# A slot table for the experts: six indirect scatters to DRAM and one load in place of products of one-hot maps

## The reference

```
probs = softmax(hf @ w_router)
topv, topi = top_k(probs, 2);  topv = topv / sum(topv)
gates = sum(one_hot(topi, 8) * topv[..., None], axis=1)
for e in range(8):
    out = out + gates[:, e:e+1] * swiglu(hf, w_gu_e[e], w_down_e[e])
swiglu(h) = (silu(g) * u) @ w_down,  g, u = split(h @ w_gu)      # w_gu 1024 x 5632, w_down 2816 x 1024
```

## Time and profile before

| | |
|---|---|
| median of 3 runs | 1412.44 us (1411.51 to 1413.75) |
| span of the profiled execution, first to last instruction | 1408.6 us |
| mean granted TensorE clock | 0.986 of full |
| PE busy | 1351.2 us, 96% of the span |
| DVE, ACT, POOL busy | 1117.5 (79%), 811.1 (58%), 238.1 (17%) us |
| share of TensorE in the chain that ended last | 88% |

### The profile page before, as it was taken

One profiled execution on the slowest core, in us unless ns is written; L12 is line 12 of the kernel. 1 busy time (PEld: TensorE's weight loads), 2 busy tenths in 40 slices (PEclk: granted clock), 3 DMA queues, 4 the chain that ended last, 5 costly groups with the idle time before them and its releaser, 6 DMA issues.

```text
span 1408.6 us, 17000 instructions
## 1 busy us (share of the span) xinstructions
PE 1351.2 (96%) x6717; PEld 1126.3 (80%) x6717; DVE 1117.5 (79%) x1031; ACT 811.1 (58%) x812; POOL 238.1 (17%) x338
## 2 busy tenths in 40 slices
PE   4999989999999998989999999999999999999996
PEld 2787557799999986788888888888888888888884
DVE  2698766567676656658899899998998999989997
ACT  4432764423232224255777777777777777767773
POOL 4000681000000013001999200000000000000001
PEclk9999999999999999989999999999999999999998
DMA  9967444854554437537899999999999999999991
GB/s 312 378 228 268 134 144 163 312 196 151 180 179 163 166 147 245 196 135 290 288 401 388 363 412 371 381 388 355 414 375 372 412 348 397 386 355 406 369 413 53
DMA packets 119238, 409.75 MB, mean 291 GB/s; under 512 B 8385, under 2 KB 31090, under 8 KB 102258
## 3 DMA queue, kind: packets, MB, share of 16 engines
q1 hardware_dynamic: 111376, 382.24, 72.2%
q0 software_dynamic: 6704, 23.14, 5.4%
q10 hardware_dynamic: 1074, 3.23, 0.6%
HBM read 398.58 MB, written 9.99 MB: 290 GB/s over the span
## 4 chain that ended last, share of the span: by engine, by line
PE 88%; POOL 4%; DVE 3%; DMA 2%; ACT 1%; issue 1%; SPq 1%; POOLq 0%; DVEq 0%; ACTq 0%
PE ps L1814 26%; PE ps L1816 26%; PE ps L1815 26%; DMA raw<-in_ada_w 2%; PE ps L2196 1%; POOL xn L725 1%; POOL o_rstd L723 1%; DVE ring_lo L1612 1%; PE ps L2096 1%; POOL o_msq L721 1%; PE ps L2038 1%; PE ps L2139 1%; SPq L502 1%; PE ps L2169 1%; DMA gbc<-in_cache_v 0%
## 5 line engine op out<-in xcount | busy, mean ns | idle before, releaser
L1612 DVE TENSOR_TENSOR ring_lo<-raw,ring_hi 128x2048 fp32r<-128x2048 f32 (+1 forms) x210 | 451.9, 2168 | 49.2 <-ACT ring_hi L1048 48.5
L1048 ACT ACTIVATE ring_hi<-raw 128x2048 fp32r<-128x2048 f32 (+1 forms) x210 | 381.3, 1820 | 123.8 <-PE ps L1816 122.8
L1814 PE MATMUL ps<-ring_hi,xe 128*128 128x512 f32 x536 | 212.1, 396 | 1.3 <-DVE xe L1663 0.8
L1816 PE MATMUL ps<-ring_lo,xe 128*128 128x512 f32 x536 | 209.8, 391 | 0.0
L1815 PE MATMUL ps<-ring_hi,xe 128*128 128x512 f32 x536 | 209.3, 390 | 0.0
L824 ACT ACTIVATE ring_hi<-raw 128x2048 fp32r<-128x2048 f32 x52 | 99.3, 1914 | 168.3 <-PE ps L1816 156.1
L1192 DVE TENSOR_TENSOR ring_lo<-raw,ring_hi 128x2048 fp32r<-128x2048 f32 x52 | 118.2, 2288 | 83.6 <-ACT ring_hi L824 83.4
L1612 DVE TENSOR_TENSOR ring_lo_more<-raw,ring_hi_more 128x2048 fp32r<-128x2048 f32 (+1 forms) x70 | 151.8, 2168 | 16.7 <-ACT ring_hi_more L1048 16.5
L1048 ACT ACTIVATE ring_hi_more<-raw 128x2048 fp32r<-128x2048 f32 (+1 forms) x70 | 127.3, 1819 | 40.1 <-PE ps L1816 39.7
L1814 PEld LDWEIGHTS ps<-ring_hi,xe 128*128 128x128 f32 x536 | 101.4, 189 | 21.9 <-DVE xe L1663 0.9
L1816 PEld LDWEIGHTS ps<-ring_lo,xe 128*128 128x128 f32 x536 | 101.0, 188 | 21.5
(11 more groups left out here) (325 smaller groups left out, 2428.8 us busy)
## 6 DMA issues: line engine op xcount, KB each, us to landing
raw<-in_w_gu_e SPq DMA_DIRECT2D x128, 1024.0 KB, 8.1
raw<-in_w_down_e SPq DMA_DIRECT2D x88, 1024.0 KB, 9.0
raw<-in_w_gu_e SPq DMA_DIRECT2D x64, 768.0 KB, 6.9
raw<-in_ada_w SPq DMA_DIRECT2D x40, 1024.0 KB, 5.5
raw<-in_w_gu SPq DMA_DIRECT2D x44, 512.0 KB, 4.9
raw<-in_w_qkv SPq DMA_DIRECT2D x12, 1024.0 KB, 8.1
raw<-in_w_down SPq DMA_DIRECT2D x11, 1024.0 KB, 5.2
raw<-in_ada_w SPq DMA_DIRECT2D x16, 512.0 KB, 13.6
```

What stands on the lines that cost most here:

```text
L1048: act.activation(ehi[m % RINGM][:, 0:w], raw[:, (MOE_U0 + m) % RAW, 0:w], ACT.Copy).then_inc(hi_ready, 1)
L1612: dve.tensor_tensor(elo[m % RINGM][:, 0:w], raw[:, (MOE_U0 + m) % RAW, 0:w], ehi[m % RINGM][:, 0:w].bitcast(F32), ALU.subtract).then_inc(l ...
L1814: pe.matmul(out, l_hi, r_hi, start=first, stop=False)
L1816: return pe.matmul(out, l_hi, r_lo, start=False, stop=last)
```

## The change

The slots' numbers no longer come from matmuls. VectorE works out for each token and each of its two choices the index of its slot, place x 8 + expert (`slots()`, right behind `select(0)`), and GpSimd scatters the pair (token number, gate) of 8 bytes to that index of a table in DRAM, `slot_dram`: one indirect DMA of 128 rows for each of three token tiles and two choices. It waits until all six have landed and loads the first 1024 entries as `filled`, 128 x 8 x 2. The table was filled before with entries for an empty slot (`blank`, one store at the end of the dense SwiGLU). `numbers_out()` reads `filled`. Of the one-hot maps only that of expert 0 and that of the last expert remain, the latter built at m = 0. `number_slots` and its 24 matmuls are gone. The constants (`pidx`, `vals`, `pairs`, `blank`) are made in `rows_of_waves()`, `vals` shrinks to two columns per token tile.

```diff
@@ VectorE
+                link(dve.tensor_tensor_reduce(o_junk[:], ident[:], iota[:], 1.0, 0.0, ALU.mult, ALU.add, pidx[:]))
+                for k in range(TILES):
+                    dve.tensor_scalar(vals[:, k, :], pidx[:].to_broadcast([P, 2]), float(P * k + 1), None, ALU.add)
+                    dve.tensor_scalar(pairs[:, k, :, 0], pidx[:].to_broadcast([P, 2]), float(P * k), None, ALU.add)
+                dve.memset(blank[:, :, 1], 0.0)
+                dve.tensor_scalar(blank[:, :, 0], pidx[:].to_broadcast([P, N_EXP]), float(TOK), None,
+                                  ALU.add).then_inc(rows_known, 1)
+                dve.wait_ge(rows_known, 2)
...
-            link(dve.tensor_tensor_reduce(o_junk[:], ident[:], iota[:], 1.0, 0.0, ALU.mult, ALU.add, pidx[:]))
-            for k in range(TILES):
-                dve.tensor_scalar(vals[:, k, :, 0], pidx[:].to_broadcast([P, N_EXP]), float(P * k + 1), None, ALU.add)
-            dve.tensor_scalar(empty_to[:], pidx[:].to_broadcast([P, N_EXP]), float(TOK + 1), None, ALU.add)
...
+            def slots():
+
+                numbered = iota[:, 0:N_EXP].unsqueeze(1).to_broadcast([P, TILES, N_EXP])
+                link(dve.scalar_tensor_tensor(slot_at[:], posm[:, :, 0:N_EXP], float(N_EXP), numbered, ALU.mult, ALU.add))
+                for j in range(2):
+                    ins = dve.tensor_tensor(slot_oh[:, j], oh[:, j], slot_at[:], ALU.mult)
+                link(ins)
+                link(dve.tensor_reduce(slot_f[:], slot_oh[:].rearrange("p j t e -> p (j t) e"), AX.X, ALU.add))
+                dve.tensor_copy(slot_of[:], slot_f[:]).then_inc(slots_ready, 1)
+
-            dve.wait_ge(acc_zeroed, 64)
+            dve.wait_ge(acc_zeroed, 80)
             select(0)
-            numbers_of = ps[:, 6, 64:80].rearrange("p (e c) -> p e c", c=2)
+            slots()
             lo(1)
...
-                dve.wait_ge(idx_ps, N_EXP)
-                dve.tensor_scalar(pick_to[:, 1:N_EXP], numbers_of[:, 1:N_EXP, 0], -1.0, 0.0, ALU.add, ALU.max)
-                link(dve.scalar_tensor_tensor(send_f[:], numbers_of[:, :, 0], 0.0, empty_to[:], ALU.is_equal, ALU.mult))
-                dve.tensor_copy(slot_gate[:], numbers_of[:, :, 1])
-                dve.scalar_tensor_tensor(send_to[:], numbers_of[:, :, 0], -1.0, send_f[:], ALU.add, ALU.add).then_inc(idx_ready, 1)
+                dve.wait_ge(slot_rows, 16 * 2 * TILES + 16)
+                dve.tensor_scalar(pick_to[:], filled[:, :, 0], float(TOK - 1), None, ALU.min)
+                dve.tensor_copy(slot_gate[:], filled[:, :, 1])
+                dve.tensor_copy(send_to[:], filled[:, :, 0]).then_inc(idx_ready, 1)
...
-                if m + 1 < N_EXP:
-                    select(m + 1)
+                if m == 0:
+                    select(LAST)
@@ GpSimd
+            pool.wait_ge(rows_known, 2)
+            pool.dma_start(slots_held, blank[:].rearrange("p e c -> p (e c)")).then_inc(acc_zeroed, 16)
...
+            def send_slots():
+
+                pool.wait_ge(slots_ready, 1)
+                pool.wait_ge(acc_zeroed, 80)
+                for j in range(2):
+                    for k in range(TILES):
+                        at = TILES * j + k
+                        pool.indirect_dma_start(slot_dram, bass.IndirectOffsetOnAxis(ap=slot_of[:, at:at + 1], axis=0),
+                                                pairs[:, k, j, :], None).then_inc(slot_rows, 16)
+                pool.wait_ge(slot_rows, 16 * 2 * TILES)
+                pool.dma_start(filled[:].rearrange("p e c -> p (e c)"), slots_held).then_inc(slot_rows, 16)
+
+            send_slots()
             pool.wait_ge(rows_stored, 16 * TILES)
             pool.wait_ge(idx_ready, 1)
             bring_rows(1)
             further_blocks()
@@ TensorE
-            def number_slots(e):
-
-                pe.wait_ge(sel_ready, e + 1)
-                for k in range(TILES):
-                    ins = pe.matmul(ps[:, 6, 64 + 2 * e:66 + 2 * e], choice[e][:, k, :], vals[:, k, e, :],
-                                    start=(k == 0), stop=(k == TILES - 1))
-                ins.then_inc(idx_ps, 1)
...
-            def number_others():
+            def turn_last_choice():
                 pe.wait_ge(cnt_ready, 1)
-                for e in range(N_EXP):
-                    number_slots(e)
+                pe.wait_ge(sel_ready, 2)
                 for k in range(TILES):
                     ins = pe.transpose(ps[:, 7, k * P:(k + 1) * P], selx[:, k, :], ident[:])
                 ins.then_inc(selT_ps, 1)
...
                     if n == TURN_K and (e, c) == (0, 1):
                         pe.wait_ge(selT_sb, 1)
-                        pe.wait_ge(idx_ready, 1)
```

More of the change, by code:

```diff
@@ L227, in build @@
         tg = sb("tg", [P, TILES, 2])
-        oh1 = sb("oh1", [P, TILES, N_EXP])
-        oh2 = sb("oh2", [P, TILES, N_EXP])
+        oh = sb("oh", [P, 2, TILES, N_EXP])
+        slot_f = sb("slot_f", [P, 2 * TILES])
+        slot_of = sb("slot_of", [P, 2 * TILES], I32)
+        pairs = sb("pairs", [P, TILES, 2, 2])
+        blank = sb("blank", [P, N_EXP, 2])
+        filled = sb("filled", [P, N_EXP, 2])
         mask = sb("mask", [P, TILES, N_EXP])
@@ L246, in build @@
         pidx = sb("pidx", [P, 1])
-        send_f = sb("send_f", [P, N_EXP])
-        vals = sb("vals", [P, TILES, N_EXP, 2])
+        vals = sb("vals", [P, TILES, 2])
         pick_to = sb("pick_to", [P, N_EXP], I32)
@@ L316, in rows_or_last, with hidden_parts @@
                 parts = (sb("y_hi", [P, D], F32R, q), sb("y_lo", [P, D], F32R, q))
-            with ExitStack() as q:
-                sb("skip_xg", [P, D], F32, q)
-                sel_y = sb("sel_y", [P, 2, TILES, P], F32, q)
             sb("pair_space", [P, 2, D], F32, s)
[L321 to L330, removed]
+            return pair + parts
+        def hidden_parts(s):
+            return sb("eh_hi", [P, 8, P], F32R, s), sb("eh_lo", [P, 8, P], F32R, s)
         def one_or_other(s):
@@ L339, in one_or_other, with tanh_or_slots @@
             return xe, more
+        def tanh_or_slots(s):
+            with ExitStack() as q:
+                slots = (sb("gate_of_oh", [P, 2, TILES, N_EXP], F32, q), sb("slot_at", [P, TILES, N_EXP], F32, q),
+                         sb("slot_oh", [P, 2, TILES, N_EXP], F32, q))
+            return sb("et", [P, D], F32, s), slots
         def experts(s):
-            return (first_or_last(s), rows_or_last(s), sb("et", [P, D], F32, s),
+            return (first_or_last(s), rows_or_last(s), tanh_or_slots(s),
                     sb("ring_hi_more", [P, UNIT], F32R, s), sb("ring_lo_more", [P, UNIT], F32R, s),
                     one_or_other(s),
-                    sb("eh", [P, D], F32, s), parts_or_choice(s),
-                    sb("sel", [P, 2, TILES, P], F32, s), sb("selx", [P, TILES, P], F32, s),
+                    sb("eh", [P, D], F32, s), hidden_parts(s),
+                    sb("sel", [P, 1, TILES, P], F32, s), sb("selx", [P, TILES, P], F32, s),
                     sb("selT", [P, TOK], F32R, s))
-        ((rows, acc), (xg, y_rows, y_hi, y_lo, sel_y), et, ring_hi_more, ring_lo_more, (xe, (x_tok, x_hT, x_y)),
-         eh, (eh_hi, eh_lo, sel_h), sel, selx, selT) = over(experts)
+        ((rows, acc), (xg, y_rows, y_hi, y_lo), (et, (gate_of_oh, slot_at, slot_oh)), ring_hi_more, ring_lo_more, (xe, (x_tok, x_hT, x_y)),
+         eh, (eh_hi, eh_lo), sel, selx, selT) = over(experts)
         last_hi, last_lo = xe[:, (LAST + 1) % 2, 0], xe[:, (LAST + 1) % 2, 1]
-        choice = [sel[:, 0], sel[:, 1], sel_y[:, 0], sel_y[:, 1], sel_h[:, 0], sel_h[:, 1], sel_h[:, 2], selx[:]]
+        choice = {0: sel[:, 0], LAST: selx[:]}
         ehi = [ring_hi[:, i, :] for i in range(RING)] + [ring_hi_more[:]]
@@ L785, in _ @@
             further_blocks()
-            pool.wait_ge(acc_zeroed, 64)
+            pool.wait_ge(acc_zeroed, 80)
             for e in range(2, N_EXP):
@@ L2293, in _ @@
                     for k in range(TILES):
-                        ins = pe.matmul(ps[:, 6, 0:2], sel[:, 0, k, :], vals[:, k, 0, :],
+                        ins = pe.matmul(ps[:, 6, 0:2], sel[:, 0, k, :], vals[:, k, :],
                                         start=(k == 0), stop=(k == TILES - 1))
```

26 lines of the change are left out of this document (13 added, 13 removed).

## The result

| | before | after |
|---|---|---|
| median of the runs | 1411.97 us (1410.95 to 1413.75, 4 runs) | 1430.8 us (1430.5 to 1434.8, 4 runs) |
| ratio, 95% interval | | 1.0138 (1.0123 to 1.0153): slower by 1.4%, some 19 us |
| span of the profiled execution | 1408.6 us | 1429.0 us |
| mean granted TensorE clock | 0.986 | 0.986 |

What follows compares the result with a forecast made beforehand. TensorE's stream was taken as the bound from the first expert matmul on. An earlier chunk 1 (2.88 us) plus matmuls back at full clock (1.9) gave 4.8 us: 1412.4 to 1407.6 us, chance 0.48, range 1406.0 to 1411.8.

Steps and rivals of the forecast that it cites:

- it does not keep its gain, or pays it elsewhere: Rival, chance 0.12: GpSimd's issues beside VectorE or the moved large tiles eat the gain; time then 1412.4 us.
- the clause on the large tiles that move by 32 bytes: Large tiles behind the new small ones shift in on-chip memory; unpriced, bounds nothing to the whole gain.
- again 93.4 us: Sign in the new profile: the stretch of expert 1 keeps its length of 93.4 us; longer would be wrong.
- a later start of expert 0: Sign that would prove the forecast wrong; the first expert matmul stood at 633.13 before.
- 6.21 us: Time of `number_slots` between chunks 0 and 1 of expert 0; gaining it in full plus 1.9 was a rival under 1%.
- The 2.88 us of gain: Chunk 1 of expert 0 starts at 659.26 in place of 662.14, once `hidden(0, 0)` ends.
- a precedent of 2.88 us that held: TensorE's idle before 538.05, after which the granted clock stayed at 1.00; used to take the clock as held.
- one of 4.34 that fell: TensorE's idle before 205.59, after which the granted clock was 0.50 for 3.40 us.
- the rival with a chance of 0.28: The clock falls in the 3.33 us pause before chunk 1 of expert 0: gain 3.3 us, time 1409.1, chance 0.28.
- the 3.8 us: Time around the profiled execution, between span 1408.6 and median 1412.44, taken as untouched by the change.
- The late table: Rival, chance 0.12: table after 666.1 stalls VectorE in `numbers_out` and starves TensorE at unit 11; 1412.0 to 1416.4 us.
- GpSimd beside VectorE: GpSimd's issues beside VectorE's low parts may slow VectorE too; unpriced, bounds nothing to the whole gain.

Runs made afterwards that it cites:

- experiment 5: Changed kernel with small tile `slot_f` moved behind the experts' large tiles, so every large tile keeps its address of the kernel before: 1411.11 us, ratio 0.9986.
- 3: Kernel before with only the tiles behind the experts' rings (`xe`, `eh`, `eh_hi` and what follows) moved by 32 bytes: 1432.73 us, ratio 1.0144.
- experiment 7: Changed kernel with 224 unused bytes behind the small tiles, large tiles 256 bytes from their places in the kernel before: 1410.91 us, ratio 0.9979.
- experiment 8: experiment 5 plus six matmuls of 384 columns, results unused, in TensorE's pause behind the transposes: 1408.78 us, ratio 0.9968.
- experiment 9: Kernel before with 32 unused bytes ahead of `raw`, so raw buffers, rings and all operands move together: 1412.99 us, ratio 1.0003.
- experiment 10: experiment 5 with GpSimd's load of `filled` held back until the low part of unit 10 is done: 1410.66 us, ratio 0.9984.
- experiment 4: Kernel before with two pads: `xe` moved by 64 bytes, `ring_hi_more` by 32 (not the move intended): 1429.81 us, ratio 1.0117.
- 1: Changed kernel with 32 unused bytes behind the small tiles, large tiles 64 bytes behind their places in the kernel before: 1430.36 us, ratio 1.0128.
- 6: Changed kernel with 96 unused bytes behind the small tiles, large tiles 128 bytes from their places in the kernel before: 1431.12 us, ratio 1.013.

## Why the prediction was wrong

**The failed step** is the last rival, "it does not keep its gain, or pays it elsewhere", and in it the clause on the large tiles that move by 32 bytes. It was named, and bounded by "nothing and the whole gain", 0 to 4.8 us, because no row prices it; in the sum it had no term. It measured 18.8 us in the medians (1430.8 - 1411.97) against a gain of about 2 without it, so some 20 us, four times its upper bound. The bound had no ground: a term that falls on every matmul of the stream is not bounded by what one gap can give. That an unchanged time, "Then 1412.4", was all that this rival could do was the mistake, and so was the forecast that expert 1 takes "again 93.4 us": it took 95.4. The text did say that an expert longer than 93.4 or a later start of expert 0 would prove it wrong, and both came: 95.4 us, and 639.27 in place of 633.13.

**What TensorE is busy with** The earlier trace rows was read as a constant. The reading that only TensorE's stream counts was right, and is just what makes 5 to 7 ns on each matmul so dear.

**The gap.** Chunk 1 waits for `eh_ready`, not for `number_slots`, and what is won is not 6.21 us but what `hidden(0, 0)` leaves: right. From ScalarE's high part of unit 10 to the first matmul of chunk 1 the prediction had 659.26 - 652.57 = 6.69 us, and after has 665.87 - 659.18 = 6.69. The 2.88 us of gain were taken from the chain's start of that matmul, 662.14; TensorE's records in order of time have it at 661.79, 6.99 us behind the start of the last matmul of chunk 0, and experiment 5 has 4.45: 2.54 by that view. TensorE idled 3.70 us, not 3.33. Of the difference 0.25 us is that the three transposes, whose 0.74 us came from the stretch at the lower clock, take 0.49 at the full one.

**The clock.** The forecast took it as held in the pause, between a precedent of 2.88 us that held and one of 4.34 that fell. With 3.70 to 3.73 it fell in all six profiled executions of the changed kernel that leave the pause empty (0.53 in after, 0.50 in experiment 5); of the clock, the rival with a chance of 0.28 was the true case. The precedent of 2.88 us was weaker than it looked, one execution taken for a rule. The same wait at the same place comes back in other traces, and in six of them (3, 5, 7, 8, 9, 10) the clock fell with it; in before and in experiment 4 it held. Experiment 9, TensorE and the stretch:

```profile
538.50 1.97 PE L1885 MATMUL ps<-ident,xn 128*128 128x128 f32 x8 [2.88 <-ACT xn L843]
...
538.39:541.80 3.41, 3.30 (x16) 1.97 (x20) 3.25 (x9) 1.49 (x4) 0.49 (x2) 0.50 0.42 175
```

So the length of an idle stretch alone did not decide it, and 2.88 against 3.33 could not carry the choice. The Trainium skill (TensorE: Matmul & The Clock Gate, What's actually happening) has the throttled state as the default that activity releases; the trace agrees, since the idle pause was followed by the lower clock and the filled one by 1.00 throughout. The rival's price, 1.5 us off the gain, fits the executions whose clock is low for 3 us: 3.3 us of gain forecast, 3.2 measured in the middle column of experiments 5 and 10. Where it is low for 6 us, as in experiment 7 and in after itself, the fall costs 2.9 (74.17 - 71.30), a case that the prediction did not have. With the clock held, 4.8 forecast, 4.5 measured in experiment 8.

**The span and the median.** The prediction took the 3.8 us between the profiled span of before and its median as time around the execution. In the runs after it that time is 1.8 to 1.9 us (1430.83 beside a span of 1429.0, 1409.56 beside 1407.7). So the profiled execution of before was itself some 2 us faster than its median, and the spans differ by 20.4 us where the medians differ by 18.8. The forecast, a difference, is not touched by it.

**What is added.** `slots()` 0.84 us (1.0 forecast), hidden under the wait for xe as said. The ten small operations in `rows_of_waves` about 1.0 us (1.3), and no wait of TensorE that could be laid to them. The store of `blank` nothing.

**The table.** There 4.9 us after the experts' start, at 644.1 with a start of 639.27; forecast 11 after it (644 with 633.13). The issues were 2.83 and then five of 0.95 to 0.99, 1.3 in the mean as forecast, but the landings were 2.9 and 1.9 in place of 4.1. The late table was given 0.12, and the table came 21 us before it was asked for; experiment 10 shows that even 3.5 us behind VectorE's demand it costs nothing. The rule of the Trainium skill (DMA: Bandwidth & Descriptors, Specifications) on transfers under 512 B was weighed for these 768 writes of 8 bytes; they landed in 2.1 to 6.9 us, below the 12.6 of the scatters with accumulate, so whatever it costs them is small here.

**GpSimd beside VectorE**, the other half of the failed rival, is out: experiment 5 has all of that traffic and 413 instructions in the stretch.

## What to carry to other kernels

In a kernel that TensorE bounds, a new small tile ahead of the large ones can be a change of every matmul: compare the operands' distances (mod 256 bytes of a partition) before and after, and put new small tiles behind the large ones, or pad to the next 256. When a change costs or brings time, look first at the mean time of an instruction that was not changed; if that has moved, no wait needs an explanation. A gap of some 4 us that could not be closed was worth filling here with matmuls nobody reads, with full clock ahead of it and behind it and their end no later than that of the wait. And a precedent read off one profiled execution is worth looking for in a second one before a choice hangs on it.

## What the runs showed of the hardware

- A matmul of 128 x 512 (fp32r operands) follows the one before after 226.6 to 229.3 ns when the distance of stationary and moving tile is what it was in before, a multiple of 256 bytes in a partition, and after 232 to 235 ns when it is off by 32, 64 or 128. Off by 256 it is fast. Moving both by 32 changes nothing. On this kernel it is 1.2 to 1.6%.
- With the ring as the stationary tile and 384 columns of `h_hi` moving it is 174.5 against 176.9 ns at 32 and 128, and 174.5 at 64: here 64 was enough. Why the two forms differ is open.
- `ring_hi_more` with `xe`, moved together by 32, took 230.8 ns in after where it took 228.7 in before, and `ring_lo_more` 228.0 against 227.7; moved together with all else (experiment 9) both had their old values. So a small part may hang on a neighbour in the stream, or on something other than the pair's own distance. That is open, and so is what in the memory or in TensorE's reads makes the distance matter: every run here shows that it does, none shows why.
- Behind 3.7 us of idle the granted clock was the lower one (0.50 to 0.53) for 3 us of work in experiments 5 and 10 and for some 6 in after and in 1, 6 and 7, at the same place of the same stream. Behind 2.88 us of idle ahead of the transposes of `xn` it was 1.00 in two traces and 0.50 in six.
- The first of six indirect scatters took GpSimd 2.83 us to issue, the other five 0.95 to 0.99, in after and in experiment 10 alike. It began inside VectorE's subtraction of a low part (631.25 to 633.54) and ended 0.9 us behind it. The gather at 666.82 in after (2.30 us, subtraction 665.95 to 668.24) and the one at 780.02 in before (2.86 us, subtraction 779.62 to 781.91) end 0.9 and 1.0 us behind theirs too, while the six gathers of before that began in a pause of VectorE or in the last 0.2 us of a subtraction took 1.03 to 1.08. So an issue beside such a subtraction lasted until some 0.9 us after its end; VectorE's own 2.29 us did not change.
